# The 64x64 inverses of two recurrences kept as two 32x32 diagonal blocks

## The chip, the cores and the metric

The kernel is one program for one core of a Trainium2 chip. It computes in f32. The metric is the device time of one execution in microseconds; the kernel before takes 2681.18 us, the median of three runs (2678.61 to 2682.38).

## What is computed

The reference is a model of three mixers. Two layers have a gated delta rule beside a forgetting attention and a pooling, followed by a dense feed-forward and by a mixture of experts; a second block has an RWKV-7 recurrence beside a gated linear recurrence, then cross attention and a feed-forward with a convolution. Sequence length is 512 and the model width 1024. The change touches only the two recurrences, cut here to what matters:

```
chunk_gated_delta_rule, layers 0 and 1 (6 heads, 8 chunks of C = 64 rows):
    a_mat = where(strict, einsum('bhnid,bhnjd->bhnij', kb, k) * decay, 0)
    uw = triangular_solve(a_mat + eye, rhs, lower=True, unit_diagonal=True)
    qk = where(causal, einsum('bhnid,bhnjd->bhnij', q, k) * decay, 0)
    scan over chunks: v_new = u_n - w_n S;  o_n = q_n S + qk_n v_new;  S = S l_n + k_n^T v_new
rwkv7_recurrence, the second block (8 heads), per row t:
    S = S diag(w_t) + (S a_t) b_t^T + v_t k_t^T;  y_t = S r_t
```

Both recurrences are computed in chunks of 64 rows. For each head and chunk that takes the inverse of a unit lower triangular 64x64 matrix, 6 heads times 8 chunks in each of the layers 0 and 1, 8 heads times 8 chunks in the second block.

## The kernel before

The program runs phase after phase, each a block with its own instruction order on every engine, held together by semaphores. Three stretches matter here: `dn_core_phase`, which runs once in layer 0 and once in layer 1, and `chunk_phase`, which runs once in the second block. Two heads make a pair; all 8 chunks of a pair lie in one tile of 128x512 (two halves of 64 partitions; within them two heads, four tiles of chunks, 64 columns). The core has three pairs, the chunk phase four.

*Formation.* PE forms the raw products of a pair (L2315 in the core, L1102 in the chunk phase). In the core it also forms the differences of the decay sums with two "own rows" operands for each pair (L2325). For the first pair VectorE (DVE) makes those rows (L2533), for the second ScalarE (ACT, L2489), for the third GpSimd (POOL, L2295). DVE writes the masked triangle `nt`. POOL masks its first level into `nb` (L2298, L1094), DVE adds the identity to give `xt` (L2546, L1231), PE moves the same through the identity (`first_level`, L2337, L1110), and DVE gives `x` (L2548, L1234). Since the later products need the halves of `nt` exchanged, PE moves them (`swap_halves`, L2345, L1131) and ACT writes them back (L2498, L1216).

*Levels.* `x` and its transpose `xt` grow from blocks of 2 to blocks of 64 in five further levels. A step is one level of one pair: POOL masks `nt` to the level's corner blocks (`nb`, L2306 and L1094, 128x512); PE makes 16 products of 64x64 (L2372, L1152); ACT copies them out of PSUM (`p1`, L2504, L1222); PE makes 16 squares for `x` (L2385, L1161; not in the last level) and 16 for `xt` (L2387, L1163); DVE adds both (L2568 and L2571, L1249 and L1252, each 128x512). In PE's order the products of the next step stand ahead of the squares of this one. In the core the steps are written out, and the score and value work of the forgetting attention is put between them on every engine (`forget_attention_part`). In the chunk phase the four inner levels are a loop in PE's program (`pe.Fori`, L1173), whose body is written once for the four pairs; each step in it has one dummy product (`turn_identity`, L45). The last level is written out.

*After the levels* PE makes `w` and `tz` with `xt` (L2404 and L2412 in the core, L1194 and L1201 in the chunk phase), and the scan over the chunks follows.

## Time and profile before

| | us |
|---|---|
| median of three runs | 2681.18 |
| profiled execution, first to last instruction | 2682.7 |
| core formation, layer 0 (174.0 to 195.0) | 21.0 |
| core levels, layer 0 (195.0 to 243.1) | 48.1 |
| core levels, layer 1 (886.6 to 934.8) | 48.2 |
| chunk formation (1881.0 to 1905.5) | 24.5 |
| chunk levels, `w` and `tz` (1905.5 to 1958.8) | 53.3 |

The profile shows one execution. PE is the matrix products of TensorE and PEld its weight loads; each f32 product has two records on either. Times in brackets behind a row are the idle time of the engine before it, with what ended it; "issue" means that the profile shows nothing that the engine waited for. The share of a window that an engine is busy does not say whether it is the one that sets the window's end; the idle times ahead of the first late row do.

### The profile page before, as it was taken

What the parts mean: (1) busy time and instruction counts of PE and PEld (TensorE: products, weight loads), DVE (VectorE), ACT (ScalarE), POOL (GpSimd) and SP (SyncE); (2) the same over time, 40 slices, a digit from 0 to 9 for tenths busy, and PEclk for the clock granted to TensorE, in tenths of its full rate; (3) what the DMA queues carried; (4) which work ended last, traced back from release to release, by engine and by line L of the source; (5) the groups of instructions that cost most, each with busy time, mean ns of one, the idle gap of its engine ahead of it and who ended that gap; (6) DMA issues with size and microseconds to landing.
All of it is one profiled execution on the core that took longest, in us unless ns stands there. A gap on an engine that the chain in (4) does not pass through costs nothing. (4 is left out here: it accounts for less than half of the span.)

```text
span 2682.7 us, 54750 instructions
## 1 busy us (share of the span) xinstructions
PE 2577.8 (96%) x22741; PEld 2075.7 (77%) x22741; DVE 1537.5 (57%) x1899; ACT 1213.5 (45%) x1578; POOL 322.1 (12%) x360
## 2 busy tenths in 40 slices
PE   8999999999999988999999998999999999999998
PEld 7776678888777867888888887864777797788887
DVE  6746454244484554676676666378566544564462
ACT  5646343122365553556556664355244523432232
POOL 6122000000110401011111111021410000000002
PEclk9999999999999989999999999999999999999999
DMA  4200244334230023777778776412024342334241
GB/s 141 83 10 4 64 118 112 85 94 114 72 94 21 4 57 119 279 276 280 283 275 292 275 277 237 119 36 78 2 73 133 88 133 71 87 100 109 81 112 53
DMA packets 351884, 331.12 MB, mean 123 GB/s; under 512 B 17273, under 2 KB 269525, under 8 KB 351605
## 3 DMA queue, kind: packets, MB, share of 16 engines
q1 hardware_dynamic: 348101, 317.76, 38.0%
q0 software_dynamic: 3392, 11.14, 1.1%
q8 instruction: 111, 1.82, 0.3%
q14 instruction: 40, 0.33, 0.0%
q10 hardware_dynamic: 240, 0.07, 0.0%
HBM read 317.41 MB, written 11.53 MB: 123 GB/s over the span
## 5 line engine op out<-in xcount | busy, mean ns | idle before, releaser
L3217 DVE TENSOR_TENSOR experts_w_lo<-experts_raw,experts_w_hi 128x2048 fp32r<-128x2048 f32 (+1 forms) x81 | 167.6, 2079 | 76.7 <-ACT experts_w_hi L3173 75.3
L3217 DVE TENSOR_TENSOR experts_w_lo<-raw_in_act,experts_w_hi 128x2048 fp32r<-128x2048 f32 (+1 forms) x81 | 167.0, 2078 | 57.4 <-ACT experts_w_hi L3173 56.9
L3173 ACT ACTIVATE experts_w_hi<-raw_in_act 128x2048 fp32r<-128x2048 f32 (+1 forms) x81 | 139.7, 1745 | 48.5 <-DMA raw_in_act<-in_moe_up 43.0
L3386 PE MATMUL psum<-experts_w_hi,experts_xg_lo 128*128 128x512 f32 x384 | 155.2, 404 | 4.2 <-DVE experts_w_lo L3217 3.1
L1641 PE MATMUL psum<-keep_act_hi,proj_w_lo 128*128 128x512 f32 x360 | 150.7, 418 | 0.1
L3387 PE MATMUL psum<-experts_w_lo,experts_xg_hi 128*128 128x512 f32 x384 | 150.7, 392 | 0.0
L3388 PE MATMUL psum<-experts_w_hi,experts_xg_hi 128*128 128x512 f32 x384 | 150.6, 392 | 0.0
L3173 ACT ACTIVATE experts_w_hi<-experts_raw 128x2048 fp32r<-128x2048 f32 (+1 forms) x81 | 140.4, 1742 | 14.2 <-DMA experts_raw<-in_moe_gate 9.3
L1643 PE MATMUL psum<-keep_act_hi,proj_w_hi 128*128 128x512 f32 x360 | 140.7, 391 | 0.0
L1642 PE MATMUL psum<-keep_act_lo,proj_w_hi 128*128 128x512 f32 x360 | 140.3, 390 | 0.0
L862 PE MATMUL psum<-keep_act_hi,conv_ffn_w_lo 128*128 128x512 f32 x336 | 131.9, 393 | 2.0 <-DVE conv_ffn_hid_lo L913 2.0
L862 PE MATMUL psum<-keep_act_hi,ffn_w_lo 128*128 128x512 f32 x336 | 131.3, 391 | 0.9 <-DVE ffn_hid_lo L913 0.9
L864 PE MATMUL psum<-keep_act_hi,conv_ffn_w_hi 128*128 128x512 f32 x336 | 131.5, 391 | 0.0
L863 PE MATMUL psum<-keep_act_lo,conv_ffn_w_hi 128*128 128x512 f32 x336 | 131.3, 391 | 0.0
L864 PE MATMUL psum<-keep_act_hi,ffn_w_hi 128*128 128x512 f32 x336 | 130.8, 389 | 0.0
L863 PE MATMUL psum<-keep_act_lo,ffn_w_hi 128*128 128x512 f32 x336 | 130.7, 389 | 0.0
L683 ACT ACTIVATE ffn_w_hi<-ffn_raw 128x1024 fp32r<-128x1024 f32 (+1 forms) x59 | 64.2, 1134 | 70.7 <-PE psum L864 69.0
L683 ACT ACTIVATE conv_ffn_w_hi<-conv_ffn_raw 128x1024 fp32r<-128x1024 f32 (+1 forms) x59 | 64.3, 1135 | 63.7 <-PE psum L864 63.2
L922 DVE TENSOR_TENSOR keep_xT<-keep_xT,psum 128x1024 f32<-128x1024 f32 x14 | 17.1, 1221 | 131.6 <-PE psum L864 131.6
L3386 PEld LDWEIGHTS psum<-experts_w_hi,experts_xg_lo 128*128 128x128 f32 x384 | 72.8, 189 | 23.3 <-issue 5.8
L1641 PEld LDWEIGHTS psum<-keep_act_hi,proj_w_lo 128*128 128x128 f32 x360 | 67.6, 188 | 25.9 <-issue 12.6
L3388 PEld LDWEIGHTS psum<-experts_w_hi,experts_xg_hi 128*128 128x128 f32 x384 | 72.7, 189 | 15.8
(856 smaller groups left out, 6779.8 us busy)
## 6 DMA issues: line engine op xcount, KB each, us to landing
raw_in_act<-in_moe_gate SPq DMA_DIRECT2D x33, 1024.0 KB, 7.4
experts_raw<-in_moe_up SPq DMA_DIRECT2D x32, 1024.0 KB, 10.3
experts_raw<-in_moe_down SPq DMA_DIRECT2D x32, 768.0 KB, 11.5
raw_in_act<-in_moe_down SPq DMA_DIRECT2D x32, 768.0 KB, 7.3
conv_ffn_raw<-in_w_ffn_in SPq DMA_DIRECT2D x43, 512.0 KB, 5.0
experts_raw<-in_moe_gate SPq DMA_DIRECT2D x17, 1024.0 KB, 8.7
raw_in_act<-in_moe_up SPq DMA_DIRECT2D x16, 1024.0 KB, 5.3
proj_raw<-in_w_in SPq DMA_DIRECT2D x18, 768.0 KB, 4.4
```

What stands on the lines that cost most here:

```text
L683: act.activation(jobs[j].view(w_hi[slot], q), raw_view(j, i, k, q), ACT.Copy).then_inc(rounded, 1)
L862: pe.matmul(out, lo[:, t, cols], x_hi, start=begin, stop=False)
L863: pe.matmul(out, hi[:, t, cols], x_lo, start=False, stop=False)
L864: last = pe.matmul(out, hi[:, t, cols], x_hi, start=False, stop=end)
L1641: pe.matmul(out, lo, m.act_hi[:, x, :], start=x == 0, stop=False)
L1642: pe.matmul(out, hi, m.act_lo[:, x, :], start=False, stop=False)
L1643: last = pe.matmul(out, hi, m.act_hi[:, x, :], start=False, stop=x == DT - 1)
L3173: act.activation(w_hi[v % 2][:, s], raw[ring][:, 0:n], ACT.Copy).then_inc(rounded, 1)
L3217: dve.tensor_tensor(w_lo[v % 2][:, s], raw[ring_of(2 * v + q)][:, 0:n], w_hi[v % 2][:, s].bitcast(F32), ALU.subtract).then_inc(split, 1)
L3386: pe.matmul(out, lhs[1][:, first + k, :], w_hi[slot][:, cols], start=begin and k == 0, stop=False)
L3387: pe.matmul(out, lhs[0][:, first + k, :], w_lo[slot][:, cols], start=False, stop=False)
L3388: last = pe.matmul(out, lhs[0][:, first + k, :], w_hi[slot][:, cols], start=False, stop=end and k == kt - 1)
```

## The change

The 64x64 inverse is kept as two 32x32 blocks of its diagonal, and the block in the lower corner is made last. A pair's `x`, its transpose and the masked corner are tiles of 128x256: four groups of 32 partitions. The masks become 32x32, five of them. DVE copies the blocks of the lower half in place (`shift`), so that PE's `swap_halves` and ACT's copy are dropped, and DVE also transposes the 32x32 blocks (`turn`), so that PE no longer squares for the transpose and `first_level` is dropped. A step of the four levels now has 32 products and 32 squares of 32x32; the corner step has 16 products (`corner`) and 32 (`right_half`). ACT writes the left half of the full 64x64 inverse and DVE the right one. `w` and `tz` use this one.

In the chunk phase the loop in PE's program is replaced by steps written out, without the dummy products. In the core the third pair's own rows move from POOL to DVE.

```diff
--- before.py
+++ after.py
-    m.eye = persist.sb("eye", [P, CH])
+    m.eye = persist.sb("eye", [P, BLK])
+    m.top_rows = persist.sb("top_rows", [P, 1])
-    m.level = persist.sb("level", [P, 6, CH])
+    m.level = persist.sb("level", [P, 5, BLK])
...
+class Blocks:
+    places = [(k, t, 2 * half + s) for t in range(TT) for k in range(2) for half in range(2) for s in range(2)]
+    uppers = [(k, t, 2 * half) for t in range(TT) for k in range(2) for half in range(2)]
...
+    def products(self, pe, p, l, bank):
+        for k, t, q in self.places:
+            last = pe.matmul(self.at(bank, q, k, t), self.masked(p, l)[self.rows(q), k, t, :], self.x(p)[self.rows(q), k, t, :],
+                             start=True, stop=True)
+        return last
+
+    def squares(self, pe, p, bank):
+        for k, t, q in self.places:
+            last = pe.matmul(self.at(bank, q, k, t), self.xt(p)[self.rows(q), k, t, :], self.kept(p)[self.rows(q), k, t, :],
+                             start=True, stop=True)
+        return last
+
+    def corner(self, pe, p, bank):
+        for k, t, q in self.uppers:
+            last = pe.matmul(self.at(bank, q + 1, k, t), self.nt[self.rows(q), p, k, t, BLK:CH], self.x(p)[self.rows(q), k, t, :],
+                             start=True, stop=True)
+        return last
+
+    def right_half(self, pe, p, bank):
+        for k, t, q in self.uppers:
+            low = self.rows(q + 1)
+            pe.matmul(self.at(bank, q, k, t), self.kept(p)[low, k, t, :], self.xt(p)[low, k, t, :], start=True, stop=True)
+            last = pe.matmul(self.at(bank, q + 1, k, t), self.x(p)[low, k, t, :], self.m.eye[low, :], start=True, stop=True)
+        return last
+
+    def shift(self, dve, p, done):
+        for q in (1, 3):
+            dve.tensor_copy(self.nt[self.rows(q), p, :, :, 0:BLK], self.nt[self.rows(q), p, :, :, BLK:CH]).then_inc(done, 1)
+
+    def mask(self, pool, p, l):
+        return pool.tensor_tensor(self.masked(p, l), self.nt[:, p, :, :, 0:BLK], self.spread(self.m.level[:, l, :]), ALU.mult)
+
+    def begin(self, dve, p):
+        return dve.tensor_tensor(self.xt(p), self.spread(self.m.eye[:, :]), self.masked(p, 0), ALU.add)
+
+    def turn(self, dve, p, back):
+        out, src = (self.flat(self.inv, p, n) for n in ((1, 0) if back else (0, 1)))
+        return dve.transpose(out, src)
+
+    def grow(self, dve, p, bank):
+        return dve.tensor_tensor(self.x(p), self.x(p), self.one(bank), ALU.add)
+
+    def keep(self, act, p, bank):
+        return act.activation(self.kept(p), self.one(bank), ACT.Copy)
+
+    def left_half(self, act, p):
+        return act.activation(self.full[:, p, :, :, 0:BLK], self.xt(p), ACT.Copy, scale=self.m.top_rows[:, 0:1])
+
+    def join(self, dve, p, bank):
+        return dve.tensor_copy(self.full[:, p, :, :, BLK:CH], self.one(bank))
...
@@ chunk_phase, the tensor engine @@
             pe.wait_ge(masked, pairs + 1)
-            pe.wait_ge(x_new, pairs)
-            pe.wait_ge(y_kept, pairs)
-            pe.wait_ge(nt_swapped, pairs)
-            products(0)
-            with pe.Fori(0, L - 2) as i:
-                for p in range(pairs):
-                    pe.wait_ge(masked, i * pairs + (pairs + p + 2))
-                    pe.wait_ge(xt_new, i * pairs + (pairs + p - 1))
-                    pe.wait_ge(p1_kept, i * pairs + (p + 1))
-                    turn_identity(m, pe, ps[:, (p + 1) % 4, 0:P], 1)
-                    products(p + 1)
-                    squares(p)
-            for n in range((L - 2) * pairs, (L - 1) * pairs):
-                if n + 1 < (L - 1) * pairs:
+            pe.wait_ge(x_new, 1)
+            products(0, 1)
+            for n in range(STEPS):
+                if n + 1 < STEPS:
                     pe.wait_ge(masked, pairs + n + 2)
-                    products(n + 1)
-                pe.wait_ge(xt_new, pairs + n - 1)
+                    pe.wait_ge(x_new, n + 2)
+                    products(n + 1, 1 + (n + 1) // pairs)
+                else:
+                    pe.wait_ge(x_new, n + 2)
+                    corner(n + 1)
                 pe.wait_ge(p1_kept, n + 1)
-                squares(n, last_level=True)
-
+                squares(n)
             for p in range(pairs):
-                pe.wait_ge(xt_new, step_of(L - 1, p))
+                n = STEPS + p
+                if p + 1 < pairs:
+                    pe.wait_ge(x_new, n + 2)
+                    corner(n + 1)
+                pe.wait_ge(p1_kept, n + 1)
+                pe.wait_ge(xt_new, n + 1)
+                blocks.right_half(pe, p, 4 + n % 4).then_inc(x_full, 1)
+
...
@@ dn_core_phase, vector, gpsimd, tensor and scalar engine @@
+            for k in range(2):
+                dve.tensor_scalar(own(2, k), r.rhs_rows[0:HD, :], r.row_of_head[0:HD, 4 + k:5 + k], None, ALU.mult).then_inc(own_2, 1)
...
-                dve.tensor_tensor(xt[:, p], eight(m.eye[:, :]), nb[:, p], ALU.add).then_inc(xt_new, 1)
-                dve.wait_ge(p1_full, p + 1)
-                dve.tensor_tensor(x[:, p], eight(m.eye[:, :]), one(6 + p % 2), ALU.add).then_inc(x_new, 1)
+                blocks.begin(dve, p).then_inc(xt_new, 1)
+                dve.wait_ge(xt_new, p + 1)
+                blocks.turn(dve, p, False).then_inc(x_new, 1)
...
+                dve.wait_ge(formed, 2 * p + 1)
+                blocks.shift(dve, p, shifted)
...
-            for k in range(2):
-                pool.tensor_scalar(own(2, k), r.rhs_rows[0:HD, :], r.row_of_head[0:HD, 4 + k:5 + k], None, ALU.mult).then_inc(own_2, 1)
             for p in range(pairs):
-                pool.wait_ge(formed, 2 * p + 1)
-                pool.tensor_tensor(nb[:, p], nt[:, p], eight(m.level[:, 0, :]), ALU.mult).then_inc(masked, 1)
-            attention.gpsimd(pool, -1)
+                pool.wait_ge(shifted, 2 * p + 2)
+                blocks.mask(pool, p, 0).then_inc(masked, 1)
...
-                if p:
-                    first_level(p - 1)
-            first_level(pairs - 1)
-            for p in range(pairs):
-                swap_halves(p)
-            pe.wait_ge(nt_swapped, pairs)
+            pe.wait_ge(low, pairs)
...
-            for p in range(pairs):
-                act.wait_ge(swapped, p + 1)
-
-                act.wait_ge(masked, p + 1)
-                act.activation(nt[:, p], one(4 + p % 2), ACT.Copy).then_inc(nt_swapped, 1)
```

On PE, in the chunk phase, the program of before has this at the head of the loop, whose body goes on with 15 more such pairs of squares and three more steps; `x`, `nb`, `xt` and `p` are the tiles named above, `keep_1_ident` is the operand of the dummy product.

```order
L1152 MATMUL psum<-chunk_3_x,chunk_2_nb 64x64 x16
L1173 UNCONDITIONAL_BRANCH
L1173 ISA
L1176 REGISTER_ALU
L1177 REGISTER_ALU
L45 MATMUL psum<-keep_1_ident 128x128
L1152 MATMUL psum<-chunk_3_x,chunk_2_nb 64x64 x16
L1161 MATMUL psum<-chunk_5_p,chunk_4_xt 64x64
L1163 MATMUL psum<-chunk_4_xt,chunk_5_p 64x64
```

In its place PE's program now has this, from the last products of the formation on; the last two rows stand in it 14 times one after the other, and the name `xt` is the tile that holds both `x` and its transpose.

```order
L1205 MATMUL psum<-recur_3_v_tok,chunk_5_p 64x64 x16
L1209 MATMUL psum<-chunk_3_x,recur_3_v_tok 64x64 x16
L1078 MATMUL psum<-chunk_4_xt,chunk_2_nb 32x32 x64
L1084 MATMUL psum<-chunk_5_p,chunk_4_xt 32x32 x32
L1078 MATMUL psum<-chunk_4_xt,chunk_2_nb 32x32 x32
```

There is no branch left between the formation and the scan, and a step is twice as many products as before for L1152 and as many as before for the squares.

On DVE, in the formation of the core, the program of before ends so (L2555 is `nt`, L2546 and L2548 are the first level):

```order
L2540 SCALAR_TENSOR_TENSOR core_5_p<-psum,keep_12_never 128x512
L2555 TENSOR_TENSOR core_1_nt<-psum,core_5_p 128x512
L2557 TENSOR_TENSOR dn_10_qb<-psum,core_5_p 128x512
L2546 TENSOR_TENSOR core_4_xt<-keep_7_eye,core_2_nb 128x512
L2548 TENSOR_TENSOR core_3_x<-keep_7_eye,psum 128x512
L2555 TENSOR_TENSOR core_1_nt<-psum,core_5_p 128x512
L2557 TENSOR_TENSOR dn_10_qb<-psum,core_5_p 128x512
```

The same place now, from the third difference on, with `shift` (L1103), the identity (L1109) and the transpose (L1113):

```order
L2578 SCALAR_TENSOR_TENSOR core_5_p<-psum,keep_13_never 128x512
L2593 TENSOR_TENSOR core_1_nt<-psum,core_5_p 128x512
L2595 TENSOR_TENSOR dn_10_qb<-psum,core_5_p 128x512
L1103 COPY core_1_nt<-core_1_nt 32x8x32 x2
L1109 TENSOR_TENSOR core_4_xt<-keep_7_eye,core_2_nb 128x256
L1113 STREAM_TRANSPOSE core_4_xt<-core_4_xt 128x256
L2593 TENSOR_TENSOR core_1_nt<-psum,core_5_p 128x512
L2595 TENSOR_TENSOR dn_10_qb<-psum,core_5_p 128x512
L1103 COPY core_1_nt<-core_1_nt 32x8x32 x2
```

The two copies of the shift stand between a pair's formation and the next pair's, and no row of DVE waits there for a product of PE that is not a raw product.

## Rows read from the trace of the kernel before

**Rows 1.** The page: PE busy us, share, instructions.

```profile
PE 2577.8 (96%) x22741; PEld 2075.7 (77%) x22741; DVE 1537.5 (57%) x1899; ACT 1213.5 (45%) x1578; POOL 322.1 (12%) x360
```

**Rows 2.** Windows: us, busy (records) of PE, PEld, DVE, ACT, POOL; PEclk, DMA, GB/s.

```profile
174.00:195.00 21.00, 16.28 (x502) 15.33 (x502) 11.86 (x18) 8.36 (x14) 13.05 (x10) 0.92 0.10 29
...
195.00:243.10 48.10, 47.34 (x1428) 38.58 (x1430) 28.14 (x70) 29.35 (x72) 22.57 (x19) 1.00 0.02 4
...
1881.00:1905.50 24.50, 20.61 (x656) 17.41 (x656) 16.21 (x24) 6.75 (x12) 9.53 (x7) 1.00 0.02 4
...
1905.50:1958.80 53.30, 50.22 (x2064) 46.27 (x2064) 25.41 (x40) 14.33 (x24) 21.62 (x17) 1.00 0.01 2
...
1918.00:1946.00 28.00, 27.46 (x1185) 25.25 (x1182) 15.17 (x24) 7.17 (x12) 14.04 (x11) 1.00 0.00 0
...
1953.75:1957.30 3.55, 2.97 (x126) 2.89 (x127) 1.38 (x2) 1.19 (x2) 0.00 (x0) 1.00 0.02 5
```

**Rows 3.** Core formation, layer 0, timeline: start, us, engine, line, [idle before].

```profile
177.97 1.56 POOL L2295 TENSOR_SCALAR core_x<-dn_rhs_rows,dn_row_of_head 64x512 f32<-64x512 f32 x1 [100.92 <-issue]
...
178.69 0.69 DVE L2555 TENSOR_TENSOR core_nt<-psum,core_p 128x512 f32<-128x512 f32 x1 [0.37 <-ACT core_p L2493]
...
181.12 0.34 PE L2325 MATMUL psum<-core_x,dn_lhs_rows 64*64 64x64 f32 x4 [2.59 <-POOL core_xt L2295]
...
189.40 2.97 PE L2345 MATMUL psum<-core_nt,keep_eye 64*64 64x64 f32 x96
...
195.00 1.15 PE L2372 MATMUL psum<-core_x,core_nb 64*64 64x64 f32 x32
```

**Rows 4.** Chunk phase by line, 1881 to 1960: busy, mean ns | idle before.

```profile
L1152 PE MATMUL psum<-chunk_x,chunk_nb 64*64 64x64 f32 x640 | 23.2, 221 | 1.0 <-ACT chunk_nt L1216 0.8 <-issue 0.2
```

**Rows 5.** DMA queues in 195 to 240 us: packets, MB, share.

```profile
q8 instruction: 11, 0.18, 1.6%
```

**Rows 6.** PE: two resumptions of the timeline; one wait of 195 to 243.

```profile
1953.77 0.40 PE L1194 MATMUL psum<-chunk_xt,recur_a_tok 64*64 64x64 f32 x12 [0.60 <-issue]
...
1957.31 0.47 PE L1194 MATMUL psum<-chunk_xt,recur_a_tok 64*64 64x64 f32 x17 [0.58 <-issue]
...
PE psum L2387 <- issue: 0.2, 1, 0.2
```

**Rows 7.** DMA rate, 1950 to 1961 us, 40 slices of 0.275 us.

```profile
GB/s 0 0 0 0 60 0 0 0 0 0 0 0 0 0 0 0 0 60 0 0 0 0 0 0 0 0 0 0 0 0 60 0 0 0 30 0 0 0 0 58
```

**Rows 8.** Timeline of PE in the chunk phase: groups of like products.

```profile
1884.91 1.98 PE L1102 MATMUL psum<-mix_rows 64*64 64x128 f32 x64 [1.72 <-DVE chunk_x L1240]
...
1888.40 0.64 PE L1123 MATMUL psum<-chunk_x,recur_v_tok 64*64 64x64 f32 x30
...
1941.15 1.09 PE L1152 MATMUL psum<-chunk_x,chunk_nb 64*64 64x64 f32 x30
```

**Rows 9.** Single operations by line: busy, mean ns | idle before.

```profile
L2211 DVE TENSOR_REDUCE core_top<-psum 128x1 f32<-128x256 f32 x4 | 1.7, 424 | 0.1
...
L2619 DVE SCALAR_TENSOR_TENSOR mix_dn<-psum,keep_params,mix_dn 128x256 f32<-128x256 f32 x2 | 0.9, 478 | 1.6 <-ACT core_p L2523 1.6
...
L2590 DVE COPY dn_a_flat<-dn_z_flat 64x384 f32<-64x384 f32 x1 | 0.3, 340 | 0.0
...
L2192 ACT ACTIVATE prob_t<-psum 128x256 f32<-128x256 f32 x2 | 0.8, 375 | 0.0
...
L2821 POOL TENSOR_SCALAR_AFFINE_SELECT route_lower<-route_lower 128x256 f32<-128x256 f32 x1 | 0.6, 642 | 0.1
```

**Rows 10.** Timeline of DVE in the chunk formation: two operations in a row.

```profile
1882.38 0.69 DVE L1240 TENSOR_TENSOR chunk_nt<-psum,keep_before 128x512 f32<-128x512 f32 x1 [2.81 <-PE psum L1102]
...
1882.98 0.68 DVE L1240 TENSOR_TENSOR qb_qb<-psum,keep_upto 128x512 f32<-128x512 f32 x1
```

**Rows 11.** Windows next to each other in the core formation (columns as in Rows 2).

```profile
178.90:182.30 3.40, 1.18 (x48) 1.18 (x52) 1.08 (x2) 0.28 (x1) 3.40 (x3) 1.00 0.02 5
182.30:185.70 3.40, 3.40 (x115) 3.40 (x106) 3.11 (x4) 0.63 (x1) 1.29 (x2) 0.51 0.02 5
```

More of the change, by code:

```diff
@@ L996, in make_masks @@
     step(pool.memset(m.eye[:, :], 0.0))
+    step(pool.memset(m.top_rows[:, :], 0.0))
     for half in halves:
         keep(m.never[half, :], 0, [[0, TT], [1, CH]], -1, fill=-1e30)
-        keep(m.eye[half, :], 0, [[-1, CH]], 1, op=ALU.not_equal, fill=1.0)
-    for l in range(6):
+        step(pool.memset(m.top_rows[half.start:half.start + BLK, :], 1.0))
+    quarters = [slice(q * BLK, (q + 1) * BLK) for q in range(P // BLK)]
+    for rows in quarters:
+        keep(m.eye[rows, :], 0, [[-1, BLK]], 1, op=ALU.not_equal, fill=1.0)
+    for l in range(5):
         b = 1 << l
-        blocks = CH // (2 * b)
+        blocks = BLK // (2 * b)
         mask = m.level[:, l, :]
         step(pool.memset(mask, 1.0))
-        for half in halves:
-            keep(m.level[half, l, :], 0, [[-2 * b, blocks], [0, 2], [0, b]], 1)
-            keep(m.level[half, l, :], b - 1, [[2 * b, blocks], [0, 2], [0, b]], -1)
+        for rows in quarters:
+            keep(m.level[rows, l, :], 0, [[-2 * b, blocks], [0, 2], [0, b]], 1)
+            keep(m.level[rows, l, :], b - 1, [[2 * b, blocks], [0, 2], [0, b]], -1)
         step(pool.memset(mask.rearrange("p (j h b) -> p j h b", h=2, b=b)[:, :, 0, :], 0.0))
@@ L1103, in form @@
                 last.then_inc(done, 1)
-            def first_level(p):
-                pe.wait_ge(masked, p + 1)
-                if p:
-                    pe.wait_ge(x_new, p)
-                for k, half, t in by_chunk:
-                    last = pe.matmul(at(4, 1 - half, k, t), nb[rows(half), p, k, t, :], m.eye[rows(half), :], start=True, stop=True)
-                last.then_inc(p1_full, 1)
             def from_v(p):
@@ L1125, in from_v @@
                 last.then_inc(y_full, 1)
-            def swap_halves(p):
-                pe.wait_ge(z_kept, p + 1)
-                for half in range(2):
-                    last = pe.matmul(ps[rows(1 - half), 5, :], m.eye[rows(half), :], nt[rows(half), p].rearrange("p k t n -> p (k t n)"),
-                                     start=True, stop=True)
-                last.then_inc(swapped, 1)
             for p in range(pairs):
@@ L1140, in _ @@
                 if p:
-                    first_level(p - 1)
                     from_v(p - 1)
-                    swap_halves(p - 1)
-            first_level(pairs - 1)
             from_v(pairs - 1)
-            swap_halves(pairs - 1)
-            def products(n):
-                p = n % pairs
-                for k, half, t in by_chunk:
-                    last = pe.matmul(at(n % 4, half, k, t), nb[rows(1 - half), p, k, t, :], x[rows(1 - half), p, k, t, :], start=True,
-                                     stop=True)
-                last.then_inc(p1_full, 1)
@@ L1156, in squares @@
-            def squares(n, last_level=False):
-                p = n % pairs
-                for k, half, t in by_chunk:
-                    if not last_level:
-                        last_x = pe.matmul(at(4 + n % 2, 1 - half, k, t), xt[rows(half), p, k, t, :], p1[rows(half), p, k, t, :], start=True,
-                                           stop=True)
-                    last = pe.matmul(at(6 + n % 2, half, k, t), p1[rows(half), p, k, t, :], xt[rows(half), p, k, t, :], start=True, stop=True)
-                if not last_level:
-                    last_x.then_inc(x_full, 1)
-                last.then_inc(xt_full, 1)
@@ L2411, in _ @@
                 for k, half, t in by_chunk:
-                    last = pe.matmul(at(2 + p % 2, half, k, t), xt[rows(half), p, k, t, :], r.z_tok[rows(half), t, cols(p, k)],
+                    last = pe.matmul(at(3 - p % 2, half, k, t), x[rows(half), p, k, t, :], r.z_tok[rows(half), t, cols(p, k)],
                                      start=True, stop=True)
```

225 lines of the change are left out of this document (122 added, 103 removed).

## The prediction

> **What bounds the kernel now.** I read the page's shares first, then the timelines of the three stretches that the change touches, then one table of windows over them, then the waits and the DMA views of the same windows. TensorE is busy 96% of the span [rows 1], so the reader should expect a gain only where PE itself gets less to do or stops waiting. The three stretches are the formation and the levels of the gated delta rule in layer 0 (174 to 243.1 us), the same in layer 1, and the chunk phase (1881 to 1958.8 us): together about 217 us. Within them PE is busy 47.34 of 48.10 us in the core levels and 50.22 of 53.30 us in the chunk levels with w and tz, but only 16.28 of 21.00 us in the core formation [rows 2].
>
> The core formation is therefore not held by PE alone. Its timeline [rows 3] shows GpSimd making the third pair's own rows from 177.97 in two operations of 1.56 us; PE waits 2.59 us for them at 181.12. Later PE moves the halves of nt (L2345, 2.97 us) and then stands until ScalarE has copied them, and the first product comes at 195.00.
>
> The second thing to see is what feeds PE with instructions. Every f32 product is recorded twice on PE and twice on the weight load: 20 groups of 16 products in the chunk phase are x640 on PE [rows 4], and the weight loads are as many as the products in every window [rows 2]. So one product is four instructions. In 195 to 240 us the instruction queue moved 11 packets, 0.18 MB, 16.4 KB each [rows 5], while PE ran 1428+1430 records in 48.1 us, that is 2674 in those 45 us, 243 a packet, and some 250 with the semaphore instructions that the records leave out. I take 256 to a packet. Now two places compared. Inside the chunk loop (1918 to 1946) no packet is moved (0 GB/s in the window's last column) although PE ran 1185+1182 records there [rows 2]: the loop's instructions stay where they are. Right behind it, where the code is straight, PE stops twice in the middle of a group of like products, 0.60 us and 0.58 us, with nothing to wait for ("issue") [rows 6]; the resumptions at 1953.77 and 1957.31 stand 3.54 us apart, with x126 and x127 records between them [rows 2], about one packet, and the queue's three packets stand 13 slices of 0.275 us, 3.58 us, apart [rows 7]. So in straight code a packet of 256 instructions is not had faster than every 3.55 us, if PE is quicker than that. In the core levels before it is not: 11.4 packets in 48.1 us is one in 4.2 us, and nearly nothing is waited for "issue" there (0.2 us) [rows 6].
>
> **The change part by part.** *Instruction counts of the levels.* Before, a step has 16 products and 32 squares, 48 products in all (32 squares become 16 in the last level). After, it has 32 and 32, each 32x32. The program of the core levels grows from 2834 PE instructions to 3794, which with about 75 semaphore instructions makes 3870, or 15.1 packets. The chunk phase has 16 steps of 64 and 4 corner steps of 48 products: 1216, times four 4864, with w and tz (128 products, 512) and semaphores 5410, or 21.1 packets; its loop is gone, all of it straight.
>
> *What PE needs for them.* Products of 64 columns start four at a time every 58 ns (30 records in 0.64 us, of which 0.22 us is the last one's length) and the old products L1152 only two at a time (30 records in 1.09 us); with 128 columns a round takes 108 ns (64 records in 1.98 us) [rows 8]. From 58 and 108 I extrapolate 33 ns for 32 columns, an estimate, bounded by 58 ns (no gain from fewer columns) and 0.5 times 58 = 29 ns. A step of 128 records is 32 rounds: 1.06 us (0.93 to 1.86), against 16+16 rounds of 58 ns = 1.86 us before. With 1.35 us of attention work in a core step (48.1 over 15 steps is 3.2, less 1.86), a core step needs PE 2.4 us (2.3 to 3.2), a chunk step 1.1 us (to 1.9). A packet is about one step (253 and 256 instructions), so at all of these values PE is quicker than 3.55 us and the packets decide.
>
> *The levels after.* I take half a packet left at the start, one packet already there, and then one each 3.55 us. Core: 0.5 x 2.4 = 1.2, then 14 x 3.55 = 49.7, and 0.6 of the last, 1.4: 52.3 us against 48.1. Chunk with w and tz: 0.6 + 20 x 3.55 + 0.7 = 72.3 us against the 53.3 us of its window before, 1905.5 to 1958.8 [rows 2].
>
> *VectorE, ScalarE, GpSimd in the levels.* DVE gives up two adds of 128x512 (0.68 us each, as [rows 10]) for one of 128x256 and a transpose of 128x256. The nearest 128x256 rows are 0.42 and 0.48 us [rows 9]; the transpose is not in this trace, and I bound it by 0.34 us (the 64x384 copy) and 1.38 us (two 128x512 operations), taking 0.48. Even at the upper end DVE needs 0.48 + 1.38 = 1.9 us of a chunk step and about 2.6 us of a core step, both under 3.55: the packets cover it; without that cover the chunk step would be DVE's. ScalarE's copy falls to 0.38 us and GpSimd's mask to about 0.64 us (the 128x256 select) [rows 9], both also covered; the corner's left half and join are one operation each per pair.
>
> *The formations.* In the core, own rows on DVE cost at most two 128x512 operations, 1.2 us, against 2 x 1.56 us on GpSimd, and stand ahead of its first work on the formation, where it waits for PE. PE's 2.59 us of waiting goes, and so do the first level (96 records), the swap (2.97 us) and ScalarE's three copies. What is late next is DVE: from its first nt at 178.69, six operations of 0.60, the third difference 0.60, three shifts of 2 x 0.30 (the nearest row, 64x384, is 0.34 [rows 9]), and begin and turn of the first pair, 2 x 0.45 (the 0.48, overlapped): 178.7 + 3.6 + 0.6 + 1.8 + 0.9, so it would have formed and shifted the third pair at 185.6, and GpSimd's two masks of 0.64 end at 186.9, where the first product can start instead of at 195.00 (PE's attention transposes, the 1.9 us ahead of 195.00, lie beside DVE's work then): -8.1 us. With shifts at 0 to 0.34 and the turn at 0.34 to 1.38 it is -9.9 to -6.9. In the chunk phase PE paces the formation, 20.61 of 24.50 us busy [rows 2]; after, PE has 1.98 us for the forms and 2 x 0.64 for v, 3.3 us a pair [rows 8], and DVE 4 x 0.60 (start to start [rows 10]) + 0.60 + 0.90 and waits of 0.25 between, 4.15 us: from 1882.38 four pairs end at 1899.0, a mask and the last turn at 1900.2, instead of 1905.5: -5.3 us (-7 to -2). GpSimd's masks in the setup are other selects of the same kind; its last work before the own rows ended 100.92 us ahead of them [rows 3], so that price is nothing.
>
> *The sum.* Core: 186.9 + 52.3 = 239.2 against 243.1, -3.9 us, twice -7.8. Chunk: 1900.2 + 72.3 = 1972.5 against 1958.8, +13.7. Together +5.9 us on the profiled span of 2682.7, 2688.6. The profile gives no time around the span; the median of the runs, 2681.18, lies 1.5 below it, so 2687.
>
> [...] The trace has the stall in straight code at 0.60 and 0.58 us per packet [rows 6] and no such stop in the loop, where nothing is moved [rows 2]. [...]
>
> **The rivals.**
> *A: the instructions keep up* (faster). Its mechanism is that several packets can be under way once PE asks faster, so that the 3.55 us does not stand. For it: only two such stops are in this stretch, and the queue is idle most of the time between its packets. Against it: the two stops are 3.54 us apart although only one packet was moved in it. Core step 2.4 us: 15 x 0.80 = 12 off, with -8.1 about -20 a layer; chunk about 1.2 us a step over 20 steps, with -5.3 some -29: -70, 2611. If 32 columns take as long as 64 (58 ns rounds), the core gains -8.1 twice and the chunk -12: -28, 2653. It decides from a period of 3.42 us down (0.1 us of it is 4.8 us of the sum), and shows as faster by 0.2% below 3.31 us.
> *B: the clock falls as well.* While PE was busy 1.18 of 3.40 us (178.9 to 182.3) its clock was full, and in the next 3.40 us it was 0.51, the lower of its two levels [rows 11]. After the change PE is busy perhaps 1.1 us of 3.55 in the chunk levels. At half clock a chunk step of 1.1 us becomes 2.2, still covered; what follows, w, tz and the scan's start, is not: I price it as one to four such stretches, each at no more than its own length: +3 to +14, so 2690 to 2701.
> *C: a packet comes only every 4.2 us*, the mean of the core levels before [rows 5]: +0.65 x 48 = +31, 2718. Against it stands the 3.54.
>
> **How the numbers follow.** Main case 0.68, with 3.35 to 3.85 us a packet and the formations' bounds: 2677 to 2701. A 0.20 (two thirds of it below 2650), B 0.07, C 0.05. About 0.2%, 5.4 us, is what a measurement of this kernel can tell from no change: 2675.8 to 2686.5. The main case's middle is 0.7 us above that bound, so it gives 0.36 slower, 0.29 the same and 0.03 faster. With A on the faster side and B and C on the slower: faster 0.23, same 0.29, slower 0.48. The range goes from 2652, A with slow rounds, to 2703, B's end.
>
> **What would show it.** In the profile after: the first core product near 187; core levels of about 52 us with PE idle for "issue" between groups of 256 records; 21 packets of the instruction queue 3.5 us apart in the chunk levels, where PE's busy share falls to a half or less; a transpose row under 1.4 us. I am wrong if the chunk levels take under 60 us, if the levels wait for DVE's transpose instead, or if the first core product does not come before 190.

## The result, and the profile after

The kernel after takes 2777.69 us, the median of four runs (2777.05 to 2781.42), against 2680.14 (2678.61 to 2682.38) for the kernel before on the same chip: a ratio of 1.0371 with the interval [1.0359, 1.0384]. It is slower, as the likeliest case had it, but by 97.5 us and not by 6, and outside the range of 2652 to 2703. The profiled execution (2778.01 us) has a span of 2776.2 us, 93.5 more than the one of before. That one, with its span of 2682.7 us, was slower than all four runs of before, so the two differences are not the same.

To find where 93.5 us lie I matched the records of DVE, ACT and POOL that both kernels have, in order, and read how much later each is (a minus is earlier). The second column is the kernel after; the third an experiment, `e4_after_layout`, which comes below.

| place (us in the kernel after) | after: later by (us) | e4: later by (us) |
|---|---|---|
| first row of core 0 (177) | 3.0 | 0.9 |
| behind core 0 (305) | 1.9 | -4.1 |
| end of the first feed-forward's inner part (645) | 7.6 | -4.1 |
| ahead of core 1 (865) | 9.3 | -4.7 |
| behind core 1 (990) | 10.6 | -7.0 |
| experts, after the first products (1105) | 9.1 | -10.8 |
| behind the experts (1720) | 59.3 | 39.2 |
| ahead of the chunk phase (1940) | 62.7 | 39.4 |
| behind its levels (2040) | 84.0 | 59.9 |
| the end | 93.5 | 59.9 |

Half of the loss, 50.2 us, lies in the mixture of experts, which the change doesn't touch. The chunk phase loses 21.3. The cores (from the first row to the second, from the fourth to the fifth) gain clearly only in the third column; what that is worth is said under the experiments. The rest builds up slowly everywhere.

**The experts.** First the queue that brings instructions, on the page of before:

```profile
q8 instruction: 111, 1.82, 0.3%
```

on that of after:

```profile
PE 2578.3 (93%) x23797; PEld 2048.9 (74%) x23797; DVE 1519.8 (55%) x1923; ACT 1201.4 (43%) x1578; POOL 282.5 (10%) x365
...
q8 instruction: 191, 3.13, 0.5%
```

PE is busy as long as before [rows 1], 2578.3 against 2577.8 us, so that by these sums the 93.5 us are idle time of PE. But the equal sums hide two things: the change saves PE some 22 us of work (the page of e4 has PE busy for 2555.3 us), and slower products, shown below, add as much again. PE's program grew by 17 blocks of 256 instructions (112 to 129), but the queue moved 80 packets more. The DMA view of six passes of the experts' loop, 1179.5 to 1650.3 us of after, has

```profile
q8 instruction: 54, 0.88, 0.8%
```

nine packets a pass; the same passes of before (1163.5 to 1593.2) have no such row. PE's windows over the same two stretches (columns as in [rows 2]), before:

```profile
1163.50:1593.20 429.70, 429.70 (x5035) 361.74 (x5034) 298.60 (x270) 257.90 (x235) 50.00 (x30) 1.00 0.79 282
```

and after:

```profile
1179.50:1650.30 470.80, 439.40 (x5035) 368.49 (x5035) 298.30 (x270) 257.81 (x234) 49.73 (x30) 0.98 0.73 259
```

The same 5035 records take 41.1 us longer in six passes, 6.85 a pass; 31.4 of it is idle, and 9.7 is longer busy time. The timeline of after shows one idle stretch a pass, at the point where PE's loop goes back to its head:

```profile
1226.64 2.29 DVE L3258 TENSOR_TENSOR experts_w_lo<-experts_raw,experts_w_hi 128x2048 fp32r<-128x2048 f32 x1 [5.09 <-ACT experts_w_hi L3214]
1228.85 2.28 DVE L3258 TENSOR_TENSOR experts_w_lo<-raw_in_act,experts_w_hi 128x2048 fp32r<-128x2048 f32 x1
...
1228.77 2.15 PE L3393 MATMUL psum<-raw_in_act,experts_ho 128*32 128x128 f32 x72
...
1235.97 0.66 PE L3427 MATMUL psum<-experts_w_hi,experts_xg_lo 128*128 128x512 f32 x1 [5.06 <-DVE experts_w_lo L3258]
```

The longer busy time lies right behind such a stop, where PE starts again at the lower of the two levels that these traces show for its clock, 1.00 and 0.50 (0.53 on the mean of this window, nine products in 3.45 us):

```profile
1235.97:1239.42 3.45, 3.45 (x9) 2.68 (x9) 3.10 (x6) 0.00 (x0) 2.45 (x2) 0.53 1.00 329
```

The list of waits of the six passes puts all six stops down to DVE:

```profile
PE psum L3427 <- DVE experts_w_lo L3258: 31.4, 6, 5.5
```

DVE's two rows end at 1228.93 and 1231.13, 7.0 and 4.8 us ahead of PE's first product. An engine that had long been done is not what PE waits for. The nine packets a pass are the other candidate; the experiments test it.

Why this loop? Counted in PE's program, its body is 1721 instructions, 6.72 blocks of 256. Before, it lies from block 64.10 to 70.82 (the places where PE stops for instructions fix where blocks begin): seven blocks. The longer cores stand ahead of it and move it to 68.49 to 75.21: eight blocks. The theory to test is that with seven it is read once, and with eight in every pass.

**The chunk phase.** Windows of after; the formation, the levels with `w` and `tz`, and the straight middle of them:

```profile
1943.87:1964.36 20.49, 15.15 (x513) 14.43 (x513) 15.89 (x32) 4.49 (x8) 5.82 (x8) 0.92 0.02 4
1964.36:2042.68 78.32, 44.63 (x2688) 41.83 (x2688) 17.64 (x39) 11.65 (x28) 8.58 (x13) 0.56 0.02 4
1972.00:2030.00 58.00, 30.44 (x1929) 28.52 (x1933) 13.42 (x31) 7.33 (x19) 3.61 (x5) 0.50 0.02 4
```

Against [rows 2] PE's share in the levels went from 94% to 57%, and the clock from 1.00 to 0.56 on the mean; in the straight middle it is 0.50, the lower of the two levels. The timeline shows the stop in every step, and that the same products now take 1.07 us instead of 0.70:

```profile
1968.28 0.25 PE L1084 MATMUL psum<-chunk_p,chunk_xt 32*32 32x32 f32 x3 [1.97 <-issue]
...
1968.97 0.70 PE L1084 MATMUL psum<-chunk_p,chunk_xt 32*32 32x32 f32 x59
1972.12 0.32 PE L1084 MATMUL psum<-chunk_p,chunk_xt 32*32 32x32 f32 x3 [2.45 <-issue]
...
1975.96 0.32 PE L1084 MATMUL psum<-chunk_p,chunk_xt 32*32 32x32 f32 x4 [1.80 <-issue]
1976.09 1.07 PE L1078 MATMUL psum<-chunk_xt,chunk_nb 32*32 32x32 f32 x64
1976.93 1.07 PE L1084 MATMUL psum<-chunk_p,chunk_xt 32*32 32x32 f32 x60
1979.80 0.32 PE L1084 MATMUL psum<-chunk_p,chunk_xt 32*32 32x32 f32 x4 [1.80 <-issue]
```

From 1968.28 to 1987.48 six such stops stand 3.84 us apart, with 127 or 128 matmul records from one to the next and as many of the weight load. A step has 64 products, four records each, so this is one step but for a record or two and, with its semaphore instructions, the 256 taken for one packet. The DMA view of the levels has the 21 packets of the forecast:

```profile
q8 instruction: 21, 0.34, 2.0%
```

The lines of the phase (busy, mean ns, idle before) show that nothing else is near its limit:

```profile
L1084 PE MATMUL psum<-chunk_p,chunk_xt 32*32 32x32 f32 x1024 | 20.6, 232 | 28.5 <-issue 28.5
L1106 POOL TENSOR_TENSOR chunk_nb<-chunk_nt,keep_level 128x256 f32<-128x256 f32 x20 | 14.4, 741 | 38.5 <-DVE chunk_nt L1103 21.9 <-PE psum L1078 16.6
L1113 DVE STREAM_TRANSPOSE chunk_xt<-chunk_xt 128x256 f32<-128x256 f32 x20 | 8.9, 445 | 0.7
L1116 DVE TENSOR_TENSOR chunk_xt<-chunk_xt,psum 128x256 f32<-128x256 f32 x16 | 6.7, 421 | 46.7 <-PE psum L1084 46.7
```

The transpose takes 0.45 us, inside the bounds and next to the 0.48 taken.

**The core.** Formation and levels of layer 0, windows of after:

```profile
177.38:190.94 13.56, 9.18 (x310) 8.23 (x311) 11.86 (x25) 7.11 (x11) 3.49 (x5) 1.00 0.16 42
190.94:247.99 57.05, 44.21 (x1897) 33.21 (x1897) 23.67 (x72) 26.71 (x73) 16.25 (x18) 0.79 0.02 4
```

The first product comes 13.56 us behind DVE's first row; before it came 20.64 behind it (174.36 to the 195.00 of [rows 3]), so 7.1 of the 8.1 us are there. The levels take 57.05 where 52.3 were forecast. PE's waits from 190 to 246 us:

```profile
PE psum L1078 <- issue: 6.4, 6, 2.0
PE psum L1084 <- issue: 5.0, 3, 2.5
PE psum L1078 <- POOL core_nb L1106: 2.9, 2, 2.0
```

Most is the wait for instructions, as forecast, but POOL's mask, which the prediction had covered, is waited for as well, 2.9 us.

**The dense phases.** Nothing waits in the first feed-forward, yet its products are slower. By line, 340 to 720 us of before:

```profile
L862 PE MATMUL psum<-keep_act_hi,ffn_w_lo 128*128 128x512 f32 x336 | 131.3, 391 | 0.9 <-DVE ffn_hid_lo L913 0.9
L864 PE MATMUL psum<-keep_act_hi,ffn_w_hi 128*128 128x512 f32 x336 | 130.8, 389 | 0.0
```

and of after:

```profile
L864 PE MATMUL psum<-keep_act_hi,ffn_w_lo 128*128 128x512 f32 x336 | 133.1, 396 | 0.7 <-DVE ffn_hid_lo L915 0.7
L866 PE MATMUL psum<-keep_act_hi,ffn_w_hi 128*128 128x512 f32 x336 | 132.7, 395 | 0.0
```

The smaller mask tiles of the change move every later tile of the on-chip memory: `act_hi` by 96 bytes, the weight tiles by 992 bytes a partition.

### The profile page after: what moved, and what is told of

It reads as the page before. It is cut to its first block and busy times, and to the rows that moved or that the text cites. A ratio compares the mean times of both kernels' runs of the same rounds, so it can differ in the third digit from the quotient of the medians.

```text
span 2776.2 us, 56732 instructions
## 1 busy us (share of the span) xinstructions
PE 2578.3 (93%) x23797; PEld 2048.9 (74%) x23797; DVE 1519.8 (55%) x1923; ACT 1201.4 (43%) x1578; POOL 282.5 (10%) x365
## 5 line engine op out<-in xcount | busy, mean ns | idle before, releaser
L3427 PE MATMUL psum<-experts_w_hi,experts_xg_lo 128*128 128x512 f32 x384 | 159.5, 415 | 40.8 <-DVE experts_w_lo L3258 39.6
L3427 PEld LDWEIGHTS psum<-experts_w_hi,experts_xg_lo 128*128 128x128 f32 x384 | 75.0, 195 | 61.2 <-DVE experts_w_lo L3258 41.9
```

Of the source, the lines that this page charges most:

```text
L3427: pe.matmul(out, lhs[1][:, first + k, :], w_hi[slot][:, cols], start=begin and k == 0, stop=False)
```

## The experiments

Theory P (place): the experts' loop is read again because it lies in eight blocks. Theory L (layout): the slow build-up is from the tiles' addresses. Rivals: the experts' loss is DVE's or a DMA's, and the build-up belongs to the new instructions or the clock.

**Moving the loop without the change.** PE instructions that do nothing but count a semaphore go ahead of the experts' loop: 165 in the kernel after (69.13 to 75.85, seven blocks), 128 in the kernel before (64.60 to 71.32, eight) and 256 (65.10 to 71.82, seven again).

```diff
+            for _ in range(165):
+                pe.nop().then_inc(idle, 1)
```

> The changed kernel with 165 semaphore increments more in the tensor engine's program, right ahead of the experts' loop; nothing else differs. Theory P (pages): the loop body of about 1720 instructions lies on 8 blocks of 256 instructions in the changed kernel (on 7 before), so that with the block ahead it no longer stays in the tensor engine's instruction buffer and is read again on each of 7 passes, 7 us a pass. 165 more instructions in front put it on 7 blocks again: 50 us less than the changed kernel's 2777.7, plus 0 to 7 us for the increments, 2728 to 2735 us; instruction packets from 191 to about 130; the 36.7 us that the experts' first product waits is gone. Rival W (weights): the experts' loop is late because VectorE's split of the weights (w_lo) is late there, for memory traffic or addresses; then the increments do nothing, 2778 to 2785 us, packets still about 191.

Measured: 2745.09 (2742.63 to 2752.16), 32.6 less than after, with 129 packets, its program's length. The idle stretch at the loop's head is gone. The fillers were not free: PE's first product of the loop shows

```profile
1099.08 0.79 PE L3430 MATMUL psum<-experts_w_hi,experts_xg_lo 128*128 128x512 f32 x1 [25.01 <-issue]
```

some 0.15 us for each of the 165. About 4 of the 25 us PE waits here without them too (1.14 and 2.93 us in after), so that roughly 50 of gain and 21 of cost are mixed; the expectation had 0 to 7 for them.

> The kernel before with 128 such increments at the same place; no block inverse, no other change. Theory P: the loop body, on 7 blocks before, lies on 8 now; it gets the 7 us a pass that the changed kernel has: 2680 + 50 + 0 to 6 = 2730 to 2736 us, packets from 111 to about 170. Rival W: 2680 to 2686 us, packets 112.

Measured: 2746.40 (2744.45 to 2750.30), ratio 1.0253 [1.0231, 1.0276], 175 packets, and the idle time of after in a kernel without the change:

```profile
PE psum L3389 <- DVE experts_w_lo L3218: 32.7, 6, 5.7
```

> The kernel before with 256 such increments at the same place, one whole block. Theory P: the loop lies as before within the blocks, so only the increments' own time is added: 2680 to 2690 us, packets 112; twice the increments of the run with 128 cost less than those. Rival W, or if the increments themselves were what costs: at least as slow as the run with 128.

Measured: 2715.37 (2713.20 to 2719.23), ratio 1.0131 [1.0110, 1.0151], 112 packets. With twice the fillers the kernel is 31 us faster than with 128. Its own 35 us over before are the fillers (0.14 each, net of that wait); half of them makes 18, which leaves 49 us for the eight blocks in e2. All three times missed by the fillers' price, but the order of the two is what only P gives: more code, less time, and the step is the table's 50 us. DVE's and the DMAs' work is the same in both.

**The edge.** More dummy transposes ahead of the loop, which PE makes in an idle stretch: 16 more end it at block 70.95, 28 more at 71.04, some ten instructions into the eighth block (`84` in the line below).

```diff
-            turn_identity(m, pe, ps[:, 7, 0:P], 56)
+            turn_identity(m, pe, ps[:, 7, 0:P], 72)
```

> The kernel before with 16 dummy transposes more (32 instructions) among the 56 that stand ahead of the experts' loop. By the count of the program's instructions (with an offset of 63 instructions that the stops in straight code give), the loop's 1721 instructions start 0.22 of a block into a block then and end at 0.94 of the seventh. Theory P: still 7 blocks, so only the dummies' time: 2679 to 2683 us, packets 111. Rival (any shift of the code, or the dummies, cost): as much as the run with 28 more, or about half of it.

Measured: 2680.43 (2673.25 to 2683.40), ratio 0.9995 [0.9985, 1.0004], 111 packets: free, as expected.

> The same with 28 dummy transposes more (56 instructions): the loop starts at 0.32 of a block and ends 9 instructions into an eighth. Theory P: 7 passes of 7 us lost, 2679 + 50 = 2729 us (2726 to 2734), packets about 172, for 24 instructions more than in the run with 16 dummies. Rival: 2680 to 2685 us.

Measured: 2701.81, ratio 1.0092 [1.0076, 1.0108], and from run to run between 2675.94 and 2707.74; the profiled execution was the 2675.94, with 111 packets. It is a step between 32 and 56 instructions, but not of 50 us: half a miss. The count of blocks is not sure to ten instructions, so this kernel stands on the edge itself. That the re-read does not cost its full price there, or not always, is a guess: no profile caught a slow execution, and this stays open.

**The layout.** The kernel after with the mask tiles as large as before, so that every later tile has its old address; every instruction is the same.

```diff
-    m.eye = persist.sb("eye", [P, BLK])
-    m.top_rows = persist.sb("top_rows", [P, 1])
+    eye = persist.sb("eye", [P, CH])
+    m.eye, m.top_rows = eye[:, 0:BLK], eye[:, BLK:BLK + 1]
-    m.level = persist.sb("level", [P, 5, BLK])
+    m.level = persist.sb("level", [P, 6, CH])[:, 0:5, 0:BLK]
```

> The changed kernel with the masks' tiles at their old sizes (the identity in 64 columns, the levels in 6 x 64, the new column in the identity's spare ones), so that every later tile has its old address in SBUF; the instructions are the same. Theory A (addresses): the dense phases lose 6 us (first feed-forward), 8 us (last one) and 2 to 3 us (first projection) because products whose operands lie 96 and 992 bytes lower stream at 0.229 to 0.241 us instead of 0.227: 2777.7 - 16 = 2762 us (2755 to 2768), all products of the feed-forward loop at 0.227 us apart. Rival: the slower pace comes from the clock or from memory traffic; 2775 to 2780 us, and the pace stays mixed.

Measured: 2748.47 (2744.44 to 2755.77), ratio 1.0266 [1.0240, 1.0291], 29 us less than after, more than expected. The feed-forward's lines are those of before again:

```profile
L864 PE MATMUL psum<-keep_act_hi,ffn_w_lo 128*128 128x512 f32 x336 | 131.2, 391 | 0.9 <-DVE ffn_hid_lo L915 0.9
L866 PE MATMUL psum<-keep_act_hi,ffn_w_hi 128*128 128x512 f32 x336 | 130.7, 389 | 0.0
```

and the windows of its first core, levels and formation, are near the prediction's:

```profile
188.63:241.31 52.68, 43.37 (x1897) 32.16 (x1898) 23.58 (x72) 26.97 (x74) 16.59 (x18) 0.84 0.02 5
175.21:188.63 13.42, 9.09 (x309) 8.14 (x310) 11.86 (x25) 7.11 (x11) 3.48 (x5) 1.00 0.15 44
```

The table's third column leaves two losses alone, the experts (50.0) and the chunk phase (20.5). L holds: only the addresses differ between e4 and after, and PE's busy time falls from 2578.3 to 2555.3 us. By which mechanism an address slows a product was not tried; the clock in the feed-forward is 1.00 with either layout.

The 52.68 us of levels next to the forecast's 52.3 are not a test that the core passed. Four profiles have the new cores (after, e1, e4, f1), two cores each. In all eight the first product comes 13.4 to 13.7 us behind DVE's first row, against 20.3 to 21.8 in the eight profiles that have the cores of before (before, e2, e3, g1, g2, c1, c2, e5). But the levels, up to the first product of `w`, take 52.7 to 59.1 us, 56.2 on the mean, against 47.4 to 48.8; e4's first core is the shortest of the eight, and its second takes 55.0. From DVE's first row to its last `mix_dn` both cores together take 227.6 (e4), 234.1 (after), 234.3 (e1) and 236.4 us (f1); with the old cores that is 226.2 to 235.0. So e4's gain of 7.3 us is no more than unchanged cores differ by: c1's are 6.4 us shorter than those of before.

> The changed kernel with its tiles at the old addresses and with 40 dummy transposes fewer ahead of the experts' loop (80 instructions), which puts the loop on 7 blocks. If the account of the loss is complete (experts' loop 50, addresses 30, chunk phase 20, cores together -3 to -8), 2748 - 50 = 2698 us (2693 to 2703), packets about 129, and what is left over the kernel before is the chunk phase. Rival: without the dummies the loop begins at the lower clock or something else of the change costs in the experts' loop; above 2710 us.

This is e4 with 40 dummy transposes fewer ahead of the loop (`56` to `16` in the line above), 68.18 to 74.90, seven blocks. Measured: 2701.23 (2698.04 to 2707.74), ratio 1.0070 [1.0054, 1.0087], 128 packets. The account closes: about 20 of 97 us are left, the size of the chunk phase's loss, and nothing is left over for a gain of the cores. In the profiled execution, the slowest of the four, core 1 gave back 8 us between its formation and its end. What makes a core vary so from one execution to the next was not settled.

**The chunk phase by itself.** The kernel before with the new chunk phase alone, straight:

```diff
+class Blocks:
...
-            with pe.Fori(0, L - 2) as i:
+            for n in range(STEPS):
...
```

> The kernel before with the chunk phase alone taken from the changed kernel (its small masks copied by GpSimd inside the phase, so that the cores, all SBUF addresses outside the phase and the tensor engine's code ahead of it stay as before). Theory F (instruction packets set the straight code): the chunk phase loses what it loses in the changed kernel, 19 to 20 us there from the traces, here 16 to 22 with the copies: 2679 + 19 = 2698 us (2695 to 2702), a packet every 3.8 us in the levels, PE waiting for 'issue' about 27 us, and nothing lost in the experts or the feed-forwards. Rival: the chunk phase of the changed kernel is slow because of the shifted addresses too; then this one loses under 10 us, below 2689.

Measured: 2700.77 (2697.51 to 2702.63), ratio 1.0076 [1.0064, 1.0088]: +19.5 us, as expected. Within the intervals this is the ratio of f1, 1.0070, which has nearly the same chunk phase and the new cores as well. So the new cores are worth between some 7 us less and 4 us more, and are not shown to gain anything. Then the same with three of its four levels in a loop again:

```diff
-            for n in range(STEPS):
+            with pe.Fori(0, L - 3) as i:
+                for p in range(pairs):
...
+                    products((p + 1) % pairs, 1)
+                    squares(p)
+            for n in range((L - 3) * pairs, STEPS):
```

> As the run with the chunk phase alone, but three of its four levels in a loop in the tensor engine's program (12 of 16 steps, one dummy product ahead of each step as before, and one mask buffer for all levels instead of two). Theory F: the 12 steps need no packets and take about 1.5 us each, 18 us; the rest, 2300 instructions or 9 packets, about 30 us: 48 against 53 before, with the formation's 2 to 5 us 2679 - 8 = 2671 us (2666 to 2677), that is some 27 us less than with the steps written out. Rival: VectorE's grow and turn or the single mask buffer hold the steps; then a step stays at 2.3 us or more and the run is above 2680.

Measured: 2680.99 (2677.81 to 2686.71), ratio 0.9999 [0.9988, 1.0011], 20 us less for the same products. Ten us of the levels, c1:

```profile
1915.00:1925.00 10.00, 5.24 (x359) 4.84 (x351) 2.60 (x6) 1.15 (x3) 1.45 (x2) 0.50 0.02 5
```

and c2:

```profile
1915.00:1925.00 10.00, 9.38 (x806) 8.13 (x799) 5.40 (x13) 2.30 (x6) 4.33 (x6) 1.00 0.00 0
1927.00:1957.00 30.00, 18.84 (x978) 17.77 (x966) 7.42 (x16) 6.30 (x15) 0.00 (x0) 0.66 0.01 4
```

In the loop PE runs 806 records instead of 359, at full clock, and no packet is moved; behind it, where the code is straight, c2 is about as slow as c1. The expectation of 2671 (2666 to 2677) was missed by 10 us. The tail of some 30 us was in it, but not that the loop's first pass is as slow as straight code, with four packets moved in it and none in the second: by the dummies that begin a pass it took 12.9 us (1899.15 to 1912.04) and the second 7.4, where 18 us stood for all three passes.

The reverse, the kernel before with its own chunk loop written out:

```diff
-            with pe.Fori(0, L - 2) as i:
+            for i in range(L - 2):
```

> The kernel before with the four levels of the chunk phase's loop written out, dummy products and all; 64x64 products as before. Theory F: 4230 straight instructions, 16.5 packets at 3.8 us less 1.5 there at the start: 58 us against 53.3, 2679 + 5 = 2684 us (2682 to 2688), a step 2.9 us. Rival (a branch costs and straight code is prefetched): 2674 to 2679 us, steps of 2.2 us.

Measured: 2689.08 (2681.96 to 2693.94), ratio 1.0028 [1.0017, 1.0038], 120 packets: +8 us, just over the expectation's upper end of 2688; the rival's 2674 to 2679 did not come. Thirty us of the levels:

```profile
1927.00:1957.00 30.00, 26.82 (x1059) 24.64 (x1061) 13.81 (x21) 7.22 (x13) 6.41 (x6) 1.00 0.02 4
```

In the loop PE ran 1185 and 1182 records in 28.00 us [rows 2], 256 in 3.03; written out, 256 take 3.62. The old products give PE more to do for each instruction than the 32x32 ones (12.7 ns of busy time a record in this window against 7.4 in that of c1, and there at half the clock), so less is lost, but writing the loop out wins nothing.

**The own rows alone**, in the kernel before:

```diff
-            for k in range(2):
-                pool.tensor_scalar(own(2, k), r.rhs_rows[0:HD, :], r.row_of_head[0:HD, 4 + k:5 + k], None, ALU.mult).then_inc(own_2, 1)
...
+            for k in range(2):
+                dve.tensor_scalar(own(2, k), r.rhs_rows[0:HD, :], r.row_of_head[0:HD, 4 + k:5 + k], None, ALU.mult).then_inc(own_2, 1)
```

> The kernel before with the third pair's own rows made by VectorE instead of GpSimd, nothing else. The prediction's term: the tensor engine's wait of 2.59 us at 181 goes, and with it the stretch at the lower clock behind it (some 1.5 us): 3 to 4 us a layer, 2679 - 7 = 2672 us (2669 to 2676). Rival: the swap and ScalarE's copies end at the same time for another reason; 2678 to 2680 us.

Measured: 2673.05 (2669.61 to 2675.54), ratio 0.9969 [0.9956, 0.9981], 8 us less, as expected: the one part of the change that was seen to gain by itself, and faster than both kernels. Last, this with the new chunk phase, all four levels in the loop:

> The kernel before with the changed chunk phase whose four levels are all in the loop (16 steps; the last pass makes one set of products that nobody reads), and with the third pair's own rows on VectorE in the cores. Theory F: against the run with three levels in the loop, 4 steps at 1.6 us in place of 3.8 and one packet's worth less ahead: 7 to 9 us less; with the own rows' 8 us 2681 - 15 = 2666 us (2662 to 2671), faster than both kernels. Rival: what is straight behind the loop (5.5 packets) still sets the end, as it starts to be read only when the loop is left; then 2672 us, as with the own rows alone.

Measured: 2672.71 (2665.04 to 2682.52), ratio 0.9969 [0.9958, 0.9981]. The expectation (2662 to 2671) was missed; the rival's 2672 came. It is no better than e7: with the loop the new chunk phase is worth about nothing. That the corner, `w` and `tz`, which stay straight, are the reason is the rival's account; it was not tested apart.

## Why the prediction was wrong

*The packets as the limit: right.* A packet of 256 instructions is what the runs show: six stops in a row in the kernel after have 127 or 128 records of products and as many of weight loads from one to the next, and e3 with 256 fillers moves 112 packets where before moves 111. A loop for which no packet is moved, and the packets as the limit of straight code of short products, are what c2 and c1 show (806 records of products in ten us of the loop, 359 in ten us of straight code, at a packet every 3.8 us). Rival A is out: six stops in a row stand 3.84 us apart, more than 3.55 and not less.

*The core: its formation right, its levels too short.* The first product comes some 7 us earlier after DVE's first row in every profile (forecast 8.1). The levels were forecast at 52.3 us and take 56.2 on the mean of eight. The forecast's own sum gives 56.4 with the packet at 3.84 us, which is the chunk phase's figure, in place of 3.55; POOL's mask, 2.9 us in one core, stood in it as covered. So the 3.9 us a layer that were forecast are not seen: about what the formation gains the levels lose again. That e4 has 7.3 us against the forecast 7.8 is luck, within what unchanged cores vary by.

*The chunk term: the right mechanism, too small.* Forecast +13.7, measured +21.3. The formation gained 3.9 us (24.36 before, then 20.49) and not 5.3. The levels took 78.3 and not 72.3: 20 packets at 3.84 instead of 3.55 us are 5.8 of these 6.0. I had taken 3.54 from one pair of stops at full clock [rows 6]. Rival B's lower clock came too, 0.50 in the levels, and as B had it the packets covered it there; its price behind them, 3 to 14 us, is not seen (e4 is 59.9 us late behind the levels and at the end). The lower clock is hardly what lengthens the packet: between 1968.28 and 1972.12 the products still took 0.70 us, and that one interval is 3.84 like the later ones. Why it is 3.84 here and 3.54 there stays open.

*"GpSimd's masks in the setup ... that price is nothing": not contradicted.* The first row of core 0 is 3.0 us later in after, but 0.9 later in e4 and 0.4 earlier in f1, which have the new masks too; with the old masks it is between 0.1 earlier and 1.2 later.

*The sum: the step that failed.* "Together +5.9 us on the profiled span" added three stretches and took the other 2466 us for unchanged. I had the two rows that could have warned me: the chunk loop runs without a packet [rows 2], and the change makes the straight code ahead of it longer. I didn't ask which other loop runs without packets, how near its end is to one block more, and what moves it. The experts' loop, 6.72 blocks long, ended 0.18 of a block short of an eighth before; the cores push it by 4.39 blocks, and 50 us follow (e1, e2, e3, f1). Nor did I ask what a smaller tile does to the addresses behind it: 29 us (e4). Neither was among the rivals, so the range could not hold the time. The direction was forecast from the chunk phase, which is 21 of the 97 us; for the rest it came right by luck.

*Straight code against a loop.* The loop was the faster form for products as short as these, c2 with 2681.0 us against c1 with 2700.8, and it was for the old ones too, 2681.3 against the 2689.1 of e5. The experts' loop shows that a loop can lose this: over seven blocks it ran its six passes without a packet (before, e1, e3, f1, g1), over eight it moved nine packets a pass, one more than its blocks, and PE stood 5.2 to 5.5 us in each where the loop goes back to its head (in six passes 31.4 us in after, 32.7 in e2, 31.1 in e4).

## What to carry to other kernels

When a change lengthens a program, look at every loop behind it as well as at the code itself: a loop that is not read again shows no instruction packets (none in six passes of the experts' loop before, 54 after), and how many blocks it covers depends on where it starts (seven from 64.10 on, eight from 68.49). Keep groups of short products in a loop, because in straight code PE got 256 instructions only every 3.8 us here, and PE, busy 5.24 of 10 us in c1, ran at the lower clock there as well, 0.50. Before a gain of a few us is read from one profile, see how much the same stretch varies in profiles of kernels that leave it alone. When a tile's size changes, hold the addresses of those behind it, which made 29 us here, and test the layout apart from the change.

## What the runs showed of the hardware

- A PE instruction that only counts a semaphore costs about 0.15 us (165 of them stood in a stop of 25.01 us), while 16 dummy transposes in an idle stretch cost nothing that could be measured (g1, 2680.43 us against 2681.18).
- The same products at the same clock, 1.00, took 389 (e4) or 395 ns (after) on the mean by the addresses of the tiles alone; over the program the layout made 29 us, 23.0 of them in PE's busy time.
- The profile can put a stop for instructions down to an engine: six stops, 31.4 us, stood under DVE, whose rows had ended 4.8 us or more before. The packets of the instruction queue in that window, 54 against none, tell it. Behind these stops PE also started again at the lower clock, 0.53 over the first 3.45 us, and its busy time was 9.7 us longer in the six passes; with the same tile addresses and no such stop the first product's line (L3427 in after, L3430 in e1) took 402 ns on the mean (e1), with the stops 415 (after).
